# A two-layer mixer kernel: conditioning chunks one for one among the weight chunks, the rstd ahead of the rotary angles, a low part amid the first h

## What is computed

```python
mod = silu(c) @ w_ada + b_ada                 # (2048) @ (2048 x 6144)
shift, scale, gate = split(mod, 3)
h = rmsnorm(x, norm_pre) * (1 + scale) + shift
z = h @ w_in                                  # (256 x 2048) @ (2048 x 14336)
y_conv = gb * causal_conv3(gcin * u) * silu(g_c)
y_ret = groupnorm(retention(rope(q), rope(k), v)) * silu(g_r)
o = concat(y_conv, y_ret) @ w_out             # (256 x 4096) @ (4096 x 2048)
x = x + gate * rmsnorm(o, norm_post)
```

## Time and profile before

| | |
|---|---|
| median of 3 runs | 1784.79 us (1781.05 to 1785.16) |
| profiled execution | 1783.31 us |
| its span, first to last instruction | 1781.5 us |
| PE busy | 1715.0 us (96%) |
| DVE busy | 1089.2 us (61%) |
| ACT busy | 717.5 us (40%) |
| mean granted TensorE clock | 0.992 |
| first matmul of chunk 0 | 50.10 us |

### The profile page before, as it was taken

One profiled execution on the slowest core, in us unless ns is written; L12 is line 12 of the kernel. 1 busy time (PEld: TensorE's weight loads), 2 busy tenths in 40 slices (PEclk: granted clock), 3 DMA queues, 4 the chain that ended last, 5 costly groups with the idle time before them and its releaser, 6 DMA issues.

```text
span 1781.5 us, 19019 instructions
## 1 busy us (share of the span) xinstructions
PE 1715.0 (96%) x7859; PEld 1396.1 (78%) x7859; DVE 1089.2 (61%) x1237; ACT 717.5 (40%) x806; POOL 36.8 (2%) x75
## 2 busy tenths in 40 slices
PE   4899999999999999999988999999999999999997
PEld 1576788887888888887777888888888888888785
DVE  0345666587866877677766455545555555567775
ACT  1333344434344344343335444444434444433332
POOL 3000000000000000000000000000000000000000
PEclk9999999999999999999998999999999999999999
DMA  7988755588877777687783555555555555568774
GB/s 258 344 289 284 275 190 172 185 293 269 297 252 253 274 278 266 213 315 274 279 276 118 171 189 189 189 181 184 188 191 183 192 189 169 189 212 330 276 281 151
DMA packets 223174, 414.62 MB, mean 233 GB/s; under 512 B 7392, under 2 KB 40560, under 8 KB 222320
## 3 DMA queue, kind: packets, MB, share of 16 engines
q1 hardware_dynamic: 222240, 413.17, 67.1%
q10 hardware_dynamic: 848, 0.24, 0.1%
HBM read 411.28 MB, written 2.10 MB: 232 GB/s over the span
## 4 chain that ended last, share of the span: by engine, by line
PE 70%; issue 17%; DMA 6%; DVE 4%; ACT 1%; POOL 1%; ACTq 0%; SPq 0%; DVEq 0%; POOLq 0%
PE Z L953 22%; PE Z L955 21%; PE Z L954 21%; DMA stage<-in_w_in 3%; DMA stage<-in_w_out 3%; DVE acc L622 1%; DVE w_lo L601 1%; ACT w_hi L452 1%; PE A L968 1%; PE B L991 1%; PE A L975 1%; PE A L991 1%; PE B L984 1%; PE B L1087 0%; PE A L1073 0%
## 5 line engine op out<-in xcount | busy, mean ns | idle before, releaser
L601 DVE TENSOR_TENSOR w_lo<-stage,w_hi 128x1024 fp32r<-128x1024 f32 x576 | 696.4, 1223 | 602.1 <-ACT w_hi L452 601.5
L452 ACT CAST w_hi<-stage 128x1024 fp32r<-128x1024 f32 x576 | 597.1, 1051 | 972.9 <-PE Z L955 597.7
L953 PE MATMUL Z<-w_hi,H 128*128 128x512 f32 x1792 | 707.7, 395 | 16.0 <-DVE w_lo L601 8.2
L955 PE MATMUL Z<-w_hi,H 128*128 128x512 f32 x1792 | 700.0, 391 | 0.0
L954 PE MATMUL Z<-w_lo,H 128*128 128x512 f32 x1792 | 699.5, 390 | 0.0
L953 PEld LDWEIGHTS Z<-w_hi,H 128*128 128x128 f32 x1792 | 337.4, 188 | 91.3 <-issue 9.7
L955 PEld LDWEIGHTS Z<-w_hi,H 128*128 128x128 f32 x1792 | 337.4, 188 | 71.2
L954 PEld LDWEIGHTS Z<-w_lo,H 128*128 128x128 f32 x1792 | 337.7, 188 | 68.1
L622 DVE SCALAR_TENSOR_TENSOR acc<-stage,c_silu,acc 128x512 f32<-128x512 f32 x240 | 180.2, 751 | 6.8
L953 PE MATMUL Z<-w_hi,YR 128*128 128x512 f32 x256 | 103.8, 406 | 2.2 <-DVE w_lo L601 2.2
L953 PE MATMUL Z<-w_hi,YC 128*128 128x512 f32 x256 | 100.2, 392 | 0.6 <-DVE w_lo L601 0.6
(11 more groups left out here) (129 smaller groups left out, 637.9 us busy)
## 6 DMA issues: line engine op xcount, KB each, us to landing
stage<-in_w_in SPq DMA_DIRECT2D x192, 1024.0 KB, 5.1
stage<-in_w_ada SPq DMA_DIRECT2D x96, 1024.0 KB, 5.9
stage<-in_w_out SPq DMA_DIRECT2D x64, 1024.0 KB, 7.4
stage<-in_w_in SPq DMA_DIRECT2D x64, 512.0 KB, 4.6
xt<-in_x SPq DMA_DIRECT2D x2, 1024.0 KB, 6.5
dec<-decay SPq DMA_DIRECT2D x8, 256.0 KB, 5.5
rows<-in_b_ada SPq DMA_DIRECT2D x2, 1024.0 KB, 5.0
rows<-in_norm_post SPq DMA_DIRECT2D x2, 1024.0 KB, 7.8
```

Of the source, the lines that this page charges most:

```text
L452: N.copy(w_hi[:, u % RING, :, :], stage[:, slot_of(n), 2 * h:2 * h + 2, :]).then_inc(s_hi, 1)
L601: V.tensor_tensor(w_lo[:, u % RING, :, :], stage[:, slot_of(n), 2 * h:2 * h + 2, :], w_hi[:, u % RING, :, :].bitcast(F32), ALU.subtract).t ...
L953: T.matmul(z[:, i, :], hh, wh, start=ch.first and a == 0, stop=False)
L955: ins = T.matmul(z[:, i, :], hl, wh, start=False, stop=stop)
```

## The change

Four things are written differently. (1) A table `FRONT_AFTER` says how many front chunks follow each weight chunk, in `LOADS` and on PE alike: 2, 2, 2, 2, 1, 1, 1 in group 0, then 2, 1, 1, 1, 1, 1, 1 and 2, 1, 1, 1, 0, 0, 0, where it was 2, 2, 2, 2, 0, 0, 0 in each of the three. The sum is 24 in both. (2) POOL's `rstd(1)` stands ahead of the angles. (3) ACT's two sines move from ahead of the first `h_full` into chunk 14. (4) `h_split` takes one half at a time, and for group 0 its second half stands behind `low(0, 0)`; the other calls make both halves as before.

```diff
@@ -84,6 +84,11 @@
+FRONT_AFTER = [2, 2, 2, 2, 1, 1, 1] + [2, 1, 1, 1, 1, 1, 1] + [2, 1, 1, 1, 0, 0, 0] + [0] * BLOCKS
...
@@ -108,6 +113,12 @@
+def front_at(n, i):
+
+    g, at = divmod(2 * GROUPS + sum(FRONT_AFTER[:n]) + i, 2 * GROUPS)
+    return g, at
...
@@ -128,10 +139,10 @@
         table.append(("w", n, 0))
-        if n < FRONT and c.g < GROUPS - 1 and c.b < 4:
-            for i in range(2):
-                at = 2 * c.b + i
-                front(c.g + 1, 1 - at // GROUPS, at % GROUPS)
+        if n < FRONT:
+            for i in range(FRONT_AFTER[n]):
+                g, at = front_at(n, i)
+                front(g, 1 - at // GROUPS, at % GROUPS)
     return table
...
@@ -507,9 +518,6 @@
-            act.wait_ge(s_ang, 1)
-            N.activation(sin_t[:, :, :], wide(R2)[:, 0:NT * HALF], ACT.Sin).then_inc(s_sin, 1)
-            N.activation(cos_t[:, :, :], wide(R2)[:, 0:NT * HALF], ACT.Sin, scale=0.5).then_inc(s_sin, 1)
 
             h_full(0, 0)
             for n, ch in enumerate(CH):
@@ -518,6 +526,10 @@
+                if n == AT_IN[0, 0, 0, 2]:
+                    act.wait_ge(s_ang, 1)
+                    N.activation(sin_t[:, :, :], wide(R2)[:, 0:NT * HALF], ACT.Sin).then_inc(s_sin, 1)
+                    N.activation(cos_t[:, :, :], wide(R2)[:, 0:NT * HALF], ACT.Sin, scale=0.5).then_inc(s_sin, 1)
...
@@ -717,11 +728,13 @@
             front_mods(1)
-            h_split(0, 0)
+            h_split(0, 0, 0)
 
             ada_seen = 0
             for n, ch in enumerate(CH):
                 low(n, 0)
+                if n == 0:
+                    h_split(0, 0, 1)
...
@@ -873,6 +889,7 @@
             step(G.memset(mhalf[:, :], -0.5))
+            rstd(1)
             ang, u, m = (wide(R2)[:, i * NT * HALF:(i + 1) * NT * HALF] for i in range(3))
...
@@ -896,7 +913,6 @@
             pool.sem_inc(s_ang, 1)
-            rstd(1)
             pool.wait_ge(s_sin, 2)
...
@@ -1018,10 +1034,9 @@
                 if n < FRONT and ch.g < GROUPS - 1:
-                    if ch.b < 4:
-                        for i in range(2):
-                            at = 2 * ch.b + i
-                            front_chunk(2 * (ch.g + 1) + at // GROUPS, at % GROUPS)
+                    for i in range(FRONT_AFTER[n]):
+                        g, at = front_at(n, i)
+                        front_chunk(2 * g + at // GROUPS, at % GROUPS)
```

More of the change, by code:

```diff
@@ L642, in gains, with h_split @@
                                        ALU.add, ALU.mult).then_inc(s_ga, 1)
[L644 to L652, removed]
+            def h_split(l, g, half):
+                k = 4 * g + 2 * half
+                tmp = tmp_buf(g)[:, 2 * half:2 * half + 2, :]
+                dve.wait_ge(s_tmp, 4 * (GROUPS * l + g) + 2 * half + 2)
+                V.tensor_copy(H[:, k:k + 2, 0:S], tmp).then_inc(s_hhi, 1)
+                dve.wait_ge(s_hhi, 2 * (GROUPS * l + g) + half + 1)
+                V.tensor_tensor(H[:, k:k + 2, S:2 * S], tmp, H[:, k:k + 2, 0:S].bitcast(F32), ALU.subtract)\
+                    .then_inc(s_h, 1)
             def variance(src, k):
@@ L739, in _ @@
                     diagonals()
-                    h_split(1, 0)
+                    for half in range(2):
+                        h_split(1, 0, half)
                 low(n, 1)
@@ L751, in _ @@
                         front_mods(k + 1)
-                        h_split(0, ch.g + 1)
+                        for half in range(2):
+                            h_split(0, ch.g + 1, half)
                 if ch.l == 1 and not ch.out and ch.j == 0 and ch.b == QK and ch.g > 0:
-                    h_split(1, ch.g)
+                    for half in range(2):
+                        h_split(1, ch.g, half)
                 for m, at_n in enumerate(ADA_SUM):
```

## The result

| | before | after |
|---|---|---|
| median | 1783.66 us (4 runs) | 1769.04 us (1768.21 to 1771.46, 4 runs) |
| profiled execution, its span | 1783.31, 1781.5 us | 1768.21, 1766.4 us |
| ratio to before, 95% interval | | 0.9911 (0.9897 to 0.9925) |
| chunk 0 begins | 50.10 us | 38.96 us |
| chunk 21 begins | 213.81 us | 196.65 us |

The ratio is 15.9 us (13.4 to 18.4) of 1783.66; forecast were 17.8 us, and 1767.0 for the time. In the two profiled executions chunk 0 is 11.1 us earlier, chunk 21 17.2, and the end 15.1.

A forecast was written before the change was run, and what follows sets the result against it. PE, busy 96% of the span, was taken as the bound, so time could come from its waits, half rate and prologue. 10.4 + 7.4 = 17.8 us off gave 1767.0 us on the median's footing; forecast 1763 to 1770, wider range 1761 to 1774.

The forecast's parts named there:

- The rstd: Prologue: rstd ahead of 32 angle instructions lets PE's first sum and chunk 0 begin 10.4 us earlier, bounds 8 to 12.
- The angles: POOL's angles end at 35.6 us and nothing waits for them; sines in chunk 14 are hidden, else cost 0.6 us.
- The low part amid the h: Ahead of chunk 0: the split's second half delayed the first low part by at most 0.1 us; nothing taken.
- One for one: Groups 0 to 2: single front chunks between weight chunks remove PE's waits for additions; 7.4 us gained, bounds 3.5 to 8.6.
- only moves: Front chunks' PE time, 1.90 us for two, stays the same in total: 2.9 us into group 0, out of group 2.
- The 1.8 us for chunk 17 at half rate: Chunk 17 takes 7.33 instead of 5.52 us behind the longest wait, 2.0 us; this goes with the wait.
- nothing gives the gain back: From chunk 21 on both programs are alike and PE is the bound, so the end comes about 17.8 us earlier.
- the sum of 17.8 us: Whole kernel: 10.4 us for the prologue plus 7.4 us for the front chunks' new order.
- The lock between POOL and DVE: Rival: five DVE instructions on the path each wait for an angle step, costing 2.9 us, giving 1769.9; chance 0.08.
- one for one gives nothing: Rival: the waits come back in other places, only the prologue's part is left, giving 1774.4 us; chance 0.12.
- the rstd doesn't come early: Rival: POOL's ISA row or something else holds POOL as long as before, giving 1777.4 us; chance 0.04.
- the low clock lasts: Rival: PE stays at 1.2 GHz through the next chunks, 7.4 us more each, four giving 1797 us; chance 0.03.

The follow-up runs named there:

- the first two runs: Kernel before with the rstd moved ahead of the angles, ratio 0.9942; then the same with the sines also moved into chunk 14, ratio 0.9938.
- the angles behind the split: Whole change, but POOL begins the angles only when the first h is split; ratio 0.9909 to the kernel before.
- last run: Whole change with two front chunks behind chunks 0 to 4, then single ones, plus chunk 0's cast and load earlier; ratio 0.9895 to the kernel before.
- no pairs later: Whole change with another table: two front chunks behind chunks 0 to 4, one behind 5 to 18, none behind 19 and 20; ratio 0.9904 to the kernel before.

## Why the prediction was right, and where its sizes were off

**The rstd: right.** 10.4 us were forecast, 11.1 are in the trace. PE's fourth front chunk ended at 22.23 instead of 22.69, which is 0.5 us of loads that landed sooner in this execution; counted from that end chunk 0 comes 16.7 us after it instead of 27.4, 10.7 us less. By the same count the run with rstd and sines has 10.3. The loads for k = 1 did not hold PE: from the start of its front chunks at 28.45 to the row copy behind them are 3.92 us, before the change 3.93. What the step left out is that ACT follows: chunk 0's load, which was to end almost together with the path through h, had landed at 35.1, and ACT's `h_full` and cast set the start.

**The angles: right.** Nothing waits for them. The prologue also needed the sines' move (1.9 us at chunk 0, by the first two runs), which the prediction named as "nothing waits for them now" without a price for the old place.

**The low part amid the h:** the step that says "I take nothing" was too low by about 0.3 us, since the cast's first half now ends before the split would.

**One for one: the mechanism right, the size too high.** 7.4 us were forecast; the traces give 6.0 (whole change) and 5.7 (alone). The waits came out as worked out: five for additions down to one, at chunk 15, with 5.17 us of landing (5.1 forecast) and a wait of 1.22 us (1.2). All waits of PE between chunk 0 and chunk 21 went from 8.0 to 2.7 us (the one of 0.47 at chunk 21 left out in both, one of 0.13 at chunk 8 put in), 5.4 us where the prediction had 5.6.

What failed in size is "only moves", the term at nothing for the front chunks' PE time. One that stands alone takes 1.00 us, two together 1.90, and a weight chunk that is followed by a front chunk takes 5.6 to 5.7 us from start to start, where chunks 4 and 5 in a row took 11.00 for both before. The change turns six pairs into twelve single ones: the front chunks take 0.8 us more, the weight chunks 0.6 and the sums 0.1, while the `x_columns` take 0.5 less, 0.9 us net.

The 1.8 us for chunk 17 at half rate came, but that was luck of the executions compared. In the kernel with rstd and sines, whose order of loads is the one before, chunk 17 waited 1.78 us and ran at full rate; in the one with rstd alone chunk 10 waited 2.06 us and had the half rate, and chunk 17 (1.79 us) had not. In the two traces compared the change has 6.8 - 3.6 = 3.2 us less at 0.50, which is 1.6 us. So the 6.0 us are 5.4 of waits and 1.6 of half rate, less 0.9 for the switches.

The same explains the scatter. The order before gives 162.5, 163.7 and 164.3 us for the stretch, the new one with its own table 157.7 to 158.4. Less half of the time at 0.50 the three are 160.3 to 160.7 and the five 155.8 to 156.3: the order is worth 4.0 to 4.9 us whatever pair one takes, and what is above that is the clock's part in those executions.

**From chunk 21 on: "nothing gives the gain back".** In the two traces first compared 2.1 us are given back there. "PE is the bound" leaves out that PE waits for low parts there too, at much the same places in every kernel but never equally long. From 215 to 1740 us, a wait of 10.5 us between the layers left aside, the changed kernel has 6.4 us of them, the one before 4.4 (and 0.6 for h), the one with the angles behind the split 2.8 (and 0.4):

```profile
PE Z L953 <- DVE w_lo L601: 4.4, 6, 1.9
...
PE Z L969 <- DVE w_lo L613: 6.4, 8, 2.1
...
PE Z L970 <- DVE w_lo L613: 2.8, 4, 1.7
```

That is 1.4 of the 2.1 us; the rest stays open. The stretch takes 1567.7, 1569.7 and 1568.3 us with the order before, 1566.1 to 1569.8 with the new one: the change's own trace is at the top of a range that both orders share, and from chunk 21 on the two programs are alike. A cause in the change was not found. In the two traces compared the sum of 17.8 us so missed by 0.7 too little in the prologue, 1.4 too much for one for one and 2.1 given back behind, which makes the 15.1 us at the end; 1.6 of these are half rate that other executions need not save.

**The rivals.** The lock between POOL and DVE is there with 0.1 to 0.2 us at most instead of 2.9. The Trainium skill (SBUF — State Buffer, "Who interferes with whom") has it that only some DVE instructions contend, one with two SBUF inputs among them. The row copy from PSUM took 0.69 us both ways, and there the traces agree. The gain, with two inputs in SBUF, is one that should be blocked: it was in two traces (0.26 and 0.32 us), while in others it took the 0.16 us that it takes alone, with POOL at work all through it; and in the changed kernel it ended at 34.67, ahead of POOL's step at 34.89 (POOL's spans in the profile are rough). So the trace doesn't bear out that every such pair waits for the whole of the other's instruction. That one for one gives nothing is excluded by its own run. That the rstd doesn't come early and that the low clock lasts are excluded by the trace: POOL's 16.32, and 7.39 us for chunk 0 (7.27 before).

## What to carry to other kernels

Look in every engine's queue for a short step on the path that stands behind a long one off it; the distance from its input to its start, here 16.24 to 31.88 us, is the most that it can cost. The price is less when something else on the path is later than the input: here PE's fourth front chunk, which ended at 22.69, left 10.4 of the 15.6 us. Where a queue of loads reuses a few slots in order, what counts is not how many transfers there are but which consumer frees the slot of each: from that consumer's end to the need of the new data must be more work than issue, landing and conversion take. And a wait removed is worth its length, but the half rate behind it only sometimes comes with it: compare two traces only after taking out the time at the lower level. Breaking pairs of short pieces of work into single ones costs too, here 0.9 us for six pairs.

## What the runs showed of the hardware

The half rate behind a wait of PE doesn't follow the wait's length alone. 2.01 us (before, chunk 17) and 2.06 us (rstd alone, chunk 10) were followed by a granted clock of 0.50 and a chunk of 7.3 us; 1.79 us (rstd alone, chunk 17), 1.78 us (rstd and sines, chunk 17) and 1.26 us (last run, chunk 5) were not, while 1.05 us (no pairs later, chunk 4) was. Nor does it follow what PE did just ahead alone: in the run with the angles behind the split chunk 4 waited 1.04 us behind the same two front chunks and sum over partitions, and ran at a granted clock of 1.00. What decides was not tried.
